# The second feed-forward product of a decoder layer: seven block products in place of eight

## The reference, cut to what matters

```python
n2 = _rmsnorm(h, g_mlp[i])
h = h + jnp.square(jax.nn.relu(n2 @ w_ff1[i])) @ w_ff2[i]     # 1024 -> 4096 -> 1024
n3 = _rmsnorm(h, g_ple[i])
h = h + jax.nn.sigmoid(n3 @ w_ple_gate[i]) * (p[i] @ w_ple[i])
return _rmsnorm(h, g_final)
```

## Time and profile before

| | |
|---|---|
| median of 3 runs | 1764.03 us (1763.82 to 1764.63) |
| the profiled execution's own time | 1764.5 us |
| its span | 1762.7 us, mean granted clock 0.981 |
| busy | PE 96%, PEld 75%, DVE 55%, ACT 35%, POOL 25% |
| moved | 145.38 MB, mean 82 GB/s |

### The profile page before, as it was taken

How to read it: one execution, slowest core, us unless ns; L and a number is a source line. 1 busy time by engine, 2 the same in 40 slices (tenths; PEclk the granted TensorE clock), 3 DMA queues, 4 the chain that set the end, 5 groups by cost and what they waited for, 6 DMA issues and landing times.

```text
span 1762.7 us, 21836 instructions
## 1 busy us (share of the span) xinstructions
PE 1685.5 (96%) x8536; PEld 1322.9 (75%) x8536; DVE 966.9 (55%) x1489; ACT 623.7 (35%) x979; POOL 437.4 (25%) x250
## 2 busy tenths in 40 slices
PE   5899989999899999999999899999999999999997
PEld 4658778787656666668888688888888888888886
DVE  7349999970345567654443844444434444445434
ACT  5342232222255566741143433433411211113323
POOL 2212352122210000111212654454412222222220
PEclk8999999999999999999999999999999999999999
DMA  5201113233200020004442233323462222231112
GB/s 153 81 24 40 45 50 101 89 100 104 73 1 1 1 73 1 1 1 143 143 143 72 96 99 127 110 96 120 155 227 96 96 96 96 96 108 42 42 60 96
DMA packets 101741, 145.38 MB, mean 82 GB/s; under 512 B 17072, under 2 KB 83632, under 8 KB 101648
## 3 DMA queue, kind: packets, MB, share of 16 engines
q1 hardware_dynamic: 97808, 130.45, 22.9%
q10 hardware_dynamic: 3680, 13.63, 2.1%
q0 software_dynamic: 160, 0.02, 0.1%
HBM read 107.51 MB, written 34.73 MB: 81 GB/s over the span
## 4 chain that ended last, share of the span: by engine, by line
PE 91%; DVE 3%; ACT 2%; issue 1%; POOL 1%; DMA 1%; ACTq 0%; DVEq 0%; POOLq 0%
PE ps L1832 54%; PE ps L2177 17%; PE ps L2062 3%; PE ps L2076 3%; PE ps L2027 2%; PE ps L2046 2%; PE ps L2033 2%; PE ps L1941 2%; PE ps L1889 1%; PE ps L1902 1%; PE ps L2141 1%; DVE prob_a L1563 1%; PE ps L2003 1%; DVE prob_b L1563 1%; PE ps L1860 0%
## 5 line engine op out<-in xcount | busy, mean ns | idle before, releaser
L824 POOL TENSOR_TENSOR w_lo<-w_raw,w_hi 128x1024 fp32r<-128x1024 f32 x67 | 163.7, 2445 | 530.5 <-ACT w_hi L938 530.5
L938 ACT ACTIVATE w_hi<-w_raw 128x1024 fp32r<-128x1024 f32 x67 | 70.8, 1060 | 362.1 <-PE ps L1832 315.7
L1832 PE MATMUL ps<-n_hi,w_hi 128*128 128x512 f32 x576 | 181.6, 397 | 15.8 <-POOL w_lo L824 4.6
L2177 PE MATMUL ps<-b_hi,a_hi 128*128 128x512 f32 x448 | 176.2, 393 | 5.6 <-issue 3.6
L1832 PE MATMUL ps<-n_lo,w_hi 128*128 128x512 f32 x576 | 180.5, 395 | 0.0
L1832 PE MATMUL ps<-n_hi,w_lo 128*128 128x512 f32 x576 | 180.3, 395 | 0.0
L2177 PE MATMUL ps<-b_lo,a_hi 128*128 128x512 f32 x448 | 175.0, 391 | 0.0
L2177 PE MATMUL ps<-b_hi,a_lo 128*128 128x512 f32 x448 | 174.9, 390 | 0.0
L1750 DVE TENSOR_TENSOR h<-h,ps 128x2048 f32<-128x2048 f32 x32 | 73.2, 2287 | 179.0 <-PE ps L1832 169.0
L1447 DVE TENSOR_SCALAR_CACHE_REDUCE tested<-sc,bar_i 128x384 bf16<-128x384 f32 (+2 forms) x192 | 169.0, 942 | 1.7 <-POOL sc L839 0.6
L1832 PE MATMUL ps<-hid_hi,wf_hi 128*128 128x512 f32 x512 | 157.8, 389 | 0.6 <-DVE h L1750 0.6
(11 more groups left out here) (304 smaller groups left out, 2917.8 us busy)
## 6 DMA issues: line engine op xcount, KB each, us to landing
f_raw<-in_w_ff_dram SPq DMA_DIRECT2D x32, 512.0 KB, 5.7
hid_scratch<-c_out SPq DMA_DIRECT2D x32, 512.0 KB, 3.5
w_raw<-in_w_ff_dram SPq DMA_DIRECT2D x32, 512.0 KB, 4.5
hid_lo<-hid_scratch SPq DMA_DIRECT2D x32, 512.0 KB, 5.8
w_raw<-in_w_in_dram SPq DMA_DIRECT2D x28, 512.0 KB, 3.7
gates_scratch<-stage ACTq DMA_DIRECT2D x16, 512.0 KB, 2.6
sig_ab<-gates_scratch SPq DMA_DIRECT2D x8, 1024.0 KB, 5.9
x_tok<-in_x_dram SPq DMA_DIRECT2D x8, 512.0 KB, 10.2
```

What stands on the lines that cost most here:

```text
L824: pool.tensor_tensor(lo_of(first)[:, :, :], w_raw[s][:, :, :], hi_of(first)[:, :, :].bitcast(F32), ALU.subtract).then_inc(lo_ready, 1)
L938: act.activation(hi_of(first)[:, :, :], w_raw[s][:, :, :], ACT.Copy).then_inc(hi_ready, 1)
L1832: last = pe.matmul(bank(4 * half + 2 * j + t)[0:w, :], wm, xm[:, t * HALF:(t + 1) * HALF], start=(k == 0 and a), stop=(k == total - 1 and ...
L2177: last = pe.matmul(unit_bank(u, PLACE[name]), w[o % 10][:, j, :], x[j][:, b, :], start=name in ("P1", "P2", "P5") and j == 0 and a, stop=j ...
```

## The change

The second product now runs in the same scheme. A unit is a pair of chunk halves: for chunk pair i and each half of the outputs (w = 2i, 2i + 1; `PAIRS_2` = 16), seven block products, each for two output tiles side by side (`ab`), with 2 chunks x 3 matmuls per tile, 12 in all. Nothing is copied out: after each of P1, P6, P7 and P4 VectorE adds the running sum where it stands in PSUM onto the part of the residual to which it belongs, and TensorE then goes on in the same bank. P2, P5 and P3 are added likewise. `SECONDS` is the order, `add_product` the addition. GpSimd makes all block sums of the weights there (`pair_sum`), and ScalarE's high parts stand five products ahead in seven slots, in the first product too.

The right operands are blocks and sums of blocks of the hidden activations. VectorE makes the sums in the first stage, four chained operations per unit (`block_sums`), and all seven blocks of 128x512 go to HBM and come back (1.75 MB a unit to store, not 1). High and low parts of them are made on 128x512. The residual is eight single tiles; four of them lie where the last units' results were, so they are loaded after these have been stored. Its norm takes the tiles in the order in which they are ready, p is turned behind the first gate projection, and the small products of p stand one quarter later.

```diff
-            def add_out(q):
-                half = group(1)
-                pair = h[:, 2 * q:2 * q + 2, :].rearrange("q a n -> q (a n)")
-                dve.tensor_tensor(pair, pair, bank(4 * half, 4), ALU.add).then_inc(psum_free[half], 1)
...
+        for w in range(PAIRS_2):
+            SECONDS += [(w, "P1")] + ([(w - 1, "P4")] if w else []) + [(w, "P2")] + ([(w - 1, "P3")] if w else [])
+            SECONDS += [(w, "P6"), (w, "P5"), (w, "P7")]
+        SECONDS += [(PAIRS_2 - 1, "P4"), (PAIRS_2 - 1, "P3")]
...
+        HIGH_AT = {(6 + k if i == 0 else 14 * i - 1 + 2 * k): (i + 1, k) for i in range(FFN - 1) for k in range(7)}
...
+            def pair_sum(w, j):
+                pool.wait_ge(a_lo_done, 1 + (LAST + POS_2[w - 1, name] if w else POS[UNITS_1 - 1, name]))
...
+                pool.tensor_tensor(four(s_raw[j - 1]), a, b, op).then_inc(s2_done, 1)
...
-                for ahead_o in HI_AT.get(o, ()) if o < 8 else (o + 6,):
+                for ahead_o in HI_AT.get(o, ()) if o < 8 else (o + 5,):
...
+            def block_sums(u):
+                low, high = c_out[u % 2]
+                dve.wait_ge(hid_sq, 2 * (u + 1))
...
+                dve.tensor_tensor(t_out[:, 1, :], high[:, second], low[:, second], ALU.subtract).then_inc(t_out_done, 1)
+                dve.wait_ge(t_out_done, 4 * u + 1)
...
+            def add_product(o, ab):
...
+                dve.wait_ge(p_done, 2 * o + ab + 1)
+                if (k, part.start) in latest:
+                    dve.wait_ge(added, latest[k, part.start])
+                latest[k, part.start] = add_count(w, name, ab)
+                dve.tensor_tensor(h[k][:, part], h[k][:, part], pair_bank(w, name, ab), ALU.add).then_inc(added, 1)
+
+            for o, (w, name) in enumerate(SECONDS):
+                add_product(o, 0)
+                add_product(o, 1)
+                if o == 0:
+                    hid_low(0, 4)
+                    block_sums(UNITS_1 - 1)
+                if o in (2, 4):
+                    hid_low(0, 4 + o // 2)
+                if o - 1 in HIGH_AT:
+                    hid_low(*HIGH_AT[o - 1])
...
+            def second_product(o):
...
+                for ab in range(2):
+                    if name in ("P6", "P7", "P4", "P3"):
+                        pe.wait_ge(added, add_count(w, {"P6": "P1", "P7": "P6", "P4": "P7", "P3": "P5"}[name], ab))
+                    elif name == "P1" and w >= 2:
+                        pe.wait_ge(added, add_count(w - 2, "P4", ab))
+                    elif name in ("P2", "P5") and w >= 1:
+                        pe.wait_ge(added, add_count(w - 1, "P2" if name == "P2" else "P3", ab))
```

More of the change, by code:

```diff
@@ new lines, in _, with late_sums @@
+            for o in range(LAST_2):
+                second_product(o)
+            assert at_.slabs == PLE_SLAB and at_.groups % 2 == EVEN
+            N2_ORDER = [1, 3, 0, 2, 5, 7, 4, 6]
+            half = group()
+            pe.wait_ge(added, add_count(PAIRS_2 - 1, "P4", 1))
+            def late_sums():
+                pe.wait_ge(added, 2 * LAST_2)
+                square_sums((4 * (1 - EVEN), 4 * (1 - EVEN) + 1), SQ3 + 7, sq_sum_2)
+            product(half, FULL, (KT, KT), residual, order=N2_ORDER[:KT],
+                    first_wait=lambda k: pe.wait_ge(norm_lo, N2_ORDER.index(k) + 1),
+                    after=lambda n: late_sums() if n == KT - 1 else None)
@@ L2231, in _, with feed @@
+            pe.wait_ge(root_done, 3)
+            def feed():
                 half = group()
                 product(half, FULL, (2,), lambda k: (pt_hi[:, k, :], pt_lo[:, k, :]))
+            half = group()
+            pe.wait_ge(p_loaded, 16)
+            for f in range(2):
+                for t in range(TT):
+                    last = pe.transpose(bank(4 * half + 2 * f, 2)[:, t * P:(t + 1) * P], p_tok[:, t, f * P:(f + 1) * P],
+                                        ident[:, :])
+            last.then_inc(turn_done, 1)
```

561 lines of the change are left out of this document (345 added, 216 removed).

## The result

The changed kernel took 1747.3 us (median of 4 runs, 1745.2 to 1752.6), the kernel before 1763.9 beside it: ratio 0.991, 95% interval 0.9888 to 0.9932. Measured again later, it was 1746.7 against 1764.3, 0.9898 (0.9883 to 0.9913). It is faster, as forecast, but by 17 us and not by 32; 1747.3 lies 0.3 us beyond the upper end of the range. The profiled execution took 1745.2 us, its span is 1743.4, and it is compared with the span of 1762.7 before.

A forecast was written before the change was run, and what follows sets the result against it. TensorE, busy 96% of the span, was taken to bound the kernel. Span 1762.7 - 43.5 + 8 (seam) + 1.5 (steady stage) + 2 (tail) = 1730.7, giving 1732 us, 1.8% less; range 1722 to 1747.

The forecast's parts named there:

- Removed: Second feed-forward product: 192 matmuls go at 0.2267 us each, 43.5 us, all on the path.
- The steady stage: New second product: hardly a stall, 1.5 us over the 49 pairs of low parts, between 0 and 18.
- The rival that they would not be saved: New matmuls lose the saving to changes of accumulator and weights; within 0.2% of before, chance 0.02.
- The balance to the hundredth: New second product: VectorE owes 5.43 us in the 5.44 us of two products, just balanced.
- the rival with 18 us more: Shared path or VectorE's queue paces the whole new stage: 18 us more, 1750 us, chance 0.18 (1742 to 1763).
- The seam: Between the two feed-forward products: late VectorE additions stall TensorE 7.3 us, taken as 8; 0 uncontended, 18 with full waits.
- The price of an operation with both inputs in SBUF: VectorE at the seam: 0.95 us per block sum of the first four, 1.07 for later sums and low halves.
- The transfers of the seam: Residual tiles 4 to 7 land at 1305, needed at 1305.5; level, so they do not decide the seam.
- The place of the waits: TensorE waits for additions, in the new stage's first 40 us and at the end of the stage before.
- First stage: First feed-forward product, steady part: added block sums are covered by VectorE's idle time; zero cost.
- The tail: After the second product: waits for sums of squares and before the second projection, 2 us together (0 to 4).
- The slower rival: GpSimd keeps the ports while work is queued, stretching 49 pairs of low parts: 155 us, 1887 us, chance 0.04.

The follow-up runs named there:

- last sums later: Changed kernel with refill spread, squares later and reload reordered, plus the last unit's block sums behind the third new product's additions: 1735.4 us, ratio 0.9835.
- the reload on four semaphores as well: Changed kernel with refill spread, sums of squares one k step later, and residual reload on four semaphores, tiles 4 and 6 first: 1735.4 us, ratio 0.9832.
- narrow sums: Changed kernel with the eight block sums of the seam on 8 of 512 columns, the rest left out: 1739.6 us, ratio 0.9865.
- GpSimd out of the way: Changed kernel with most of GpSimd's low parts and pair sums around the seam cut to 2 columns of each 128: 1734.9 us, ratio 0.9836.
- three versions here: Block sums moved behind the evictions in the changed kernel, 1746.5 us; in the three-edit version, last unit's sums later, 1735.4, or both units' sums later, 1735.3.

## Why the prediction was off

- **Removed.** Right. 192 matmuls are gone, the steady stage has 1104 records in 250 us at clock 1.00, and the account above closes with 43.5. The rival that they would not be saved is out.
- **The steady stage**, 1.5 us, between 0 and 18. It cost 0: 250.00 busy of 250. An addition takes 0.678 us (0.69 forecast) and the pair of low parts 2.38 in most places, where 2.95 was worked out. I had the second of a pair find a whole operation of GpSimd in front of it, 1.80 us, and that was right (1.78 in 40 of 40); the first, for which I took 1.15, took 0.69 in 29 of 40. The mean pair is 2.54. The balance to the hundredth, 5.43 in 5.44, was thus 0.4 us better, and the rival with 18 us more had nothing to stand on. That is luck as far as the first of the pair goes: nothing in the working said that it would mostly go free. VectorE was busy for 87% and TensorE never waited.
- **The seam**, 8 us. This is the step that failed: 15.0 of waits and 4.8 at the long pitch, 19.7, beyond even its bound of 18. Three of its terms failed:
  - *The price of an operation with both inputs in SBUF.* I took 0.95 us for each of the first four block sums and 1.07 for the second four. They took 1.63 to 1.78, 13.5 us for eight where my terms are 8.1. The 14 low parts of the next chunk, also 1.07 each or 15.0, took 19.0; only the four ahead of the first sums, beside an idle GpSimd, were under my price (0.67 each for 0.75). That this stretching is GpSimd's doing is shown by the run with its work taken away: 0.69 for each of the eight sums. What sets the long ones apart is their place. One that stands right behind another with both inputs in SBUF finds an operation of GpSimd in front of it and takes 1.6 to 1.8, chained (the eight sums) or independent (the second of a pair). One behind additions from PSUM mostly takes 0.69, and so did a chained sum that stood there (1296.13, last sums later). I had this in the stage itself, 1.25 + 0.55 for the second of a pair, and did not use it in the seam, where I spread a mean wait of 0.45 over all. No run made the eight sums independent; that the chain adds nothing is read from these rows.
  - *The refill behind every product.* Two additions and a pair of low parts take VectorE 3.5 us there (from 1329.37 to 1332.87), a product takes TensorE 2.72. This is the cause of the pauses at 1322, 1333 and 1347: with the refill spread, 6.5 us of them became 1.0, and none was left with the reload on four semaphores as well. My sum counted this work, at too low a price, and looked only at its end.
  - *No term for the clock.* The first three stops, of 2 to 5 us, were followed by 6 to 9 matmuls at 0.43 each: 4.8 us. I had forecast stops of this size and given them no more than their own length. The excesses named (5.4 and 4.0 us of VectorE's time, 4.8 of slow pitch) overlap with each other and with VectorE's idle time; how is not told apart.
- **The transfers of the seam** that "do not decide". I worked out 1305 for the residual's landing and 1305.5 for its need. The block sums were done at 1300.0 and not at 1292, and the additions could start at 1314.7. VectorE's idle time before them was 5.06 us, 5.66 with narrow sums, 8.73 with GpSimd out of the way; my sum as one long queue (51 us of work from 1279.3) has no room for it. But what TensorE lost by it is small in the changed kernel: with the idle time cut to 1.88 its pauses behind the second wait were 6.0 in place of 6.5. So the landing was wrong by some 10 us and the term of nothing nearly held, which is luck. With GpSimd out of the way the transfer did become a wait of 2.6 us, at 1310.
- **The place of the waits** was right in the main: for the additions, at the end of the stage before and early in the stage, though they reached 66 us into it and not 40. So was the cause, VectorE's operations with two inputs in SBUF. The Trainium skill (SBUF — State Buffer, Who interferes with whom) has that whoever issues first keeps the ports for its whole instruction; the 0.69 against 1.67 and the 8 columns that took 0.17 or 1.2 agree.
- **First stage**, 0: measured 0.4; TensorE has no gap in 1100 to 1195.
- **The tail**, 2 us (0 to 4): 4.3. The sums of squares cost 2.6 where 1 was taken, and moving them by one step took the wait away. The 0.9 ahead of the stage's last product had no term.
- **The slower rival**, GpSimd keeping the ports while it has work: out. In the eight chained sums and in the pairs the two engines took turns, at 1.7 us a turn; two of GpSimd's operations ahead of each would have made them 2.5 and more.

What stays open: how much of 5 us of slow pitch can be had back, and why the waits behind the second one divide differently from run to run. What the reload of h is worth alone in time, 0.002 in the ratio, is inside the intervals.

## What to carry to other kernels

Price an operation by what stands in front of it, not by a mean. Where two engines take turns, one that comes right behind another of its kind pays the whole turn (1.7 us here, for 0.69 of work), and one behind operations that don't take part in the turns mostly pays nothing. Then sum the queue stretch by stretch, since a stretch that owes more than its time stops TensorE wherever the whole sum ends. Where an engine is just level with a transfer, look at both orders; waits taken away ahead of it lengthened VectorE's idle time from 5 to 9 us. Moving work within the crowded queue (three versions here) only moved the stop. What did pay was taking work out of the crowded stretch (the refill spread over more products).
